# The long convolution's two VectorE accumulators in a PSUM bank in place of SBUF

## The chip, the cores and the metric

The kernel runs on one core of one Trainium2 chip. The metric is the device time of one execution in microseconds; the time before is the median of three runs. All arithmetic is float32, and every large matmul is done as three float32r passes (high times high, high times low, low times high), so that each weight needs a "high" and a "low" part made on the core.

## The reference, cut to what matters

A first block with two branches (a gated delta rule over 16 heads, and a GLU with a long depthwise convolution), then a second block of two layers. The change touches the convolution of the second branch alone:

```python
SEQ, CONV_CH, CONV_KERNEL = 256, 2048, 31
def causal_depthwise_conv(x, w):        # frame t sees t-K+1..t
    K = w.shape[0]
    xp = jnp.pad(x, ((0, 0), (K - 1, 0), (0, 0)))
    return lax.conv_general_dilated(xp, w[:, None, :], (1,), 'VALID', ..., feature_group_count=x.shape[-1])
...
u = jax.nn.glu(glu_in, axis=-1)
u = causal_depthwise_conv(u, w_dw[i]) + b_dw[i]
u = jax.nn.silu(layernorm(u, ln_g[i], ln_b[i])) * jax.nn.silu(z_b)
y_b = u @ w_br_b[i]
```

The 2048 channels are 16 groups of 128; a group lies with channels on the partitions and the 256 frames along the free dimension. Each frame is a sum of 31 products, plus the bias.

## The kernel before, in words

The kernel is a sequence of blocks. A block is one weight slab of 2048 rows by 512 columns, in 16 chunks of 128 rows, multiplied with 256 tokens (two tiles of 128). For each chunk ScalarE rounds the raw weights to `w_hi` (`hi_piece`, line 396), VectorE subtracts to get `w_lo` (`lo_piece`, line 402), and TensorE does six 512-column matmuls into one of two PSUM pairs (lines 422 to 424). ScalarE and VectorE work `AHEAD` = 6 chunks ahead of TensorE; `w_hi` holds 8 chunks, so a high piece waits for the chunk eight before it to be used. SyncE issues the weight loads of each quarter of a slab when its low pieces are made.

The order of everything else is written out by hand. A block has 32 half-steps `hs`, two to a chunk, and each engine walks them in order: at each one it does what the function for that engine lays on it and then, on VectorE, after each odd half-step one low piece. Blocks 0 to 15 are heads, blocks 16 to 31 are the convolution branch. Beside the projection of group j+1, the engines process group j (`group_pe`, `group_act`, `group_pool`, `group_dve`); group 0 runs beside the rule of head 15 as well, and group 15 beside the first block of the tail.

One group, by half-step:

- hs 0: ScalarE waits for the block's matmuls (`psum_ready`) and copies the pair to `bproj` (lines 770, 771); VectorE adds the gate bias (line 822).
- hs 1, 2: ScalarE takes the tanh of the gates (line 775); VectorE makes `glu2` and `z2b` (lines 831, 832).
- hs 5: TensorE waits for them (`glu_ready`) and transposes both into bank QA (line 760), in the midst of its stream of matmuls. ScalarE copies QA to `upad` and `zb` (lines 780, 782).
- hs 6 to 28: VectorE does 23 of the 31 taps, one per half-step, into two accumulators in turn: two `tensor_scalar` (lines 841, 843) and 21 `scalar_tensor_tensor` (line 847), each of which waits for the last write of its own accumulator. Inputs are `upad`, a tap weight per partition from `cwl`, and the accumulator.
- hs 8 to 22, even ones: ScalarE makes the other 8 products into `tap` (line 794), and GpSimd adds them up in `acc_p` with 7 `tensor_tensor` (line 815), each after the product it needs.
- hs 30, 31: VectorE adds its two accumulators (line 851), then `acc_p` (line 855), which gives `ub`. GpSimd stages the weights of the next group after line 851 (lines 806, 807).

PSUM is full: two pairs take four banks; QA and QB serve the heads' transposes, and RA and RB the rule. In the convolution blocks QA holds the transposes of hs 5. QB is last written for head 15, and next used in the norm of the tail.

Of the kernel before, what the change touches and what calls it, by code (L numbers as in the profile page):

```python
# [22 lines left out]
ALU = mybir.AluOpType  # L23
# [3 lines left out]
P = 128  # L27
D = 2048
S = 256
# [6 lines left out]
HEADS = 16  # L36
# [75 lines left out]
def program(nc, t, out, ctx):  # L112
# [16 lines left out]
    def sb(name, shape, dt=F32):  # L129

        h = nc.alloc_sbuf_tensor_at(name, shape, dt, offset=spot[0])
        spot[0] += (4 * int(np.prod(shape[1:])) + 31) // 32 * 32
        assert spot[0] <= nc.sbuf_usable_end
        return h
# [85 lines left out]
    ub = sb("ub", [P, KC, S])  # L220
# [3 lines left out]
    upad = sb("upad", [P, 2, LONG - 1 + S + 2])  # L224
# [2 lines left out]
    cwl = sb("cwl", [P, LONG + 1])  # L227
    assert spot[0] <= at_kq
    spot[0] = at_kq
    acc = sb("acc", [P, 2, S])  # L230
    glu2 = sb("glu2", [P, TT, P])
    assert spot[0] <= at_kq + 4 * TT * 3 * P
    spot[0] = at_ap
# [4 lines left out]
    acc_p = sb("acc_p", [P, S])  # L238
# [69 lines left out]
    QA, QB, RA, RB = (nc.alloc_psum_tensor(n, [P, NB], F32) for n in ("QA", "QB", "RA", "RB"))  # L308
# [6 lines left out]
    def both(x):  # L315

        return x.unsqueeze(1).broadcast_to([P, TT, P])
# [21 lines left out]
    s = {n: sem(n) for n in names}  # L339
# [11 lines left out]
    long_tap = [sem(f"long_tap{i}") for i in range(2)]  # L351
    tap_ready = [sem(f"tap_ready{i}") for i in range(2)]

    def reach(eng, which, value):

        if not isinstance(value, int) or value > 0:
            eng.wait_ge(which, value)
# [379 lines left out]
               .then_inc(s["oa_lo_done"], 1)  # L737


    POOL_TAPS = 8  # L740
    DVE_TAPS = LONG - POOL_TAPS

# [20 lines left out]
    def group_act(act, j, par, hs):  # L763
# [13 lines left out]
        if hs == 5:  # L777
# [5 lines left out]
               .then_inc(s["b_cols_taken"], 1)  # L783
        if 8 <= hs < 8 + 2 * POOL_TAPS and hs % 2 == 0:
            n = (hs - 8) // 2
# [6 lines left out]

            reach(act, s["pool_taps"], (POOL_TAPS - 1) * j + (max(n - 2, 1) if n >= 2 else 0))
            act.activation(tap[:, n % 2], upad[:, par, k:k + S], ACT.Copy, scale=cwl[:, k:k + 1])\  # L794
               .then_inc(tap_ready[n % 2], 1)

    def group_pool(pool, j, par):
# [5 lines left out]
        reach(pool, s["u_summed"], j)  # L803
        reach(pool, s["pool_taps"], (POOL_TAPS - 1) * j)
        taps = chan[:, CH_LONG:CH_END].rearrange("p (k g) -> p k g", g=KC)
        pool.tensor_copy(cwl[:, LONG:LONG + 1], chan[:, bass.ds(CH_BDW + j, 1)])
        pool.tensor_copy(cwl[:, 0:LONG], taps[:, :, bass.ds(j, 1)].rearrange("p k a -> p (k a)")).then_inc(s["cwl_staged"], 1)
        reach(pool, s["u_ready"], j)
        for n in range(1, POOL_TAPS):
            if n == 1:  # L810
                pool.wait_ge(tap_ready[0], POOL_TAPS // 2 * j + 1)
            else:
# [5 lines left out]
    def group_dve(dve, j, par, hs):  # L818
        if hs == 0:
            dve.wait_ge(psum_free, BLK_B + j + 1)  # L820
            dve.wait_ge(s["bg_loaded"], 16 * j + 16)
            dve.tensor_tensor(bproj[:, :, 3 * P:NB], bproj[:, :, 3 * P:NB], both(bg[:, :]), ALU.add)\
               .then_inc(s["gate_biased"], 1)
        if hs == 2:
            dve.wait_ge(s["b_tanh"], j + 1)
            if isinstance(j, int) and j == 0:
                dve.wait_ge(s["zs_ready"], HEADS)
                dve.wait_ge(s["oa_lo_done"], HEADS - 1)
                dve.wait_ge(s["pads_ready"], 4)
            reach(dve, s["b_cols"], j)  # L830
            dve.scalar_tensor_tensor(glu2[:, :, :], bth[:, :, 0], 1.0, bproj[:, :, 0:P], ALU.add, ALU.mult)
            dve.scalar_tensor_tensor(z2b[:, :, :], bth[:, :, 1], 1.0, bproj[:, :, 2 * P:3 * P], ALU.add, ALU.mult)\
               .then_inc(s["glu_ready"], 1)
        if 6 <= hs < 6 + DVE_TAPS:
            k = hs - 6
            src, a = upad[:, par, k:k + S], acc[:, k % 2]
            if k == 0:
                dve.wait_ge(s["b_cols_taken"], j + 1)
                dve.wait_ge(s["cwl_staged"], j + 1)
                reach(dve, s["u_ready"], j)  # L840
                dve.tensor_scalar(a, src, cwl[:, 0:1], cwl[:, LONG:LONG + 1], ALU.mult, ALU.add).then_inc(long_tap[0], 1)
            elif k == 1:
                dve.tensor_scalar(a, src, cwl[:, 1:2], None, ALU.mult).then_inc(long_tap[1], 1)
            else:
                n = (DVE_TAPS + 1 - k % 2) // 2
                dve.wait_ge(long_tap[k % 2], n * j + k // 2)
                dve.scalar_tensor_tensor(a, src, cwl[:, k:k + 1], a, ALU.mult, ALU.add).then_inc(long_tap[k % 2], 1)  # L847
        if hs == 30:
            dve.wait_ge(long_tap[0], (DVE_TAPS + 1) // 2 * (j + 1))
            dve.wait_ge(long_tap[1], DVE_TAPS // 2 * (j + 1))  # L850
            dve.tensor_tensor(acc[:, 0], acc[:, 0], acc[:, 1], ALU.add).then_inc(s["u_summed"], 1)
        if hs == 31:
            dve.wait_ge(s["u_summed"], j + 1)
            dve.wait_ge(s["pool_taps"], (POOL_TAPS - 1) * (j + 1))
            dve.tensor_tensor(ub[:, bass.ds(j, 1)].rearrange("p a n -> p (a n)"), acc[:, 0], acc_p[:, :], ALU.add)\
               .then_inc(s["u_ready"], 1)


# [789 lines left out]
    def beside_dve(dve, blk, hs):  # L1648
        at = 32 * (blk - BLK_GB) + hs
        done = blk - 1  # L1650
        if blk == BLK_GB:
            group_dve(dve, KC - 1, 1, hs)
# [275 lines left out]
    @block.vector  # L1928
    def _(dve):
        keys = lambda h, par, hs: keys_dve(dve, h, par, hs)  # L1930
        rule = lambda h, par, hs: rule_dve(dve, h, par, hs)
        group = lambda j, par, hs: group_dve(dve, j, par, hs)
        start_dve(dve)
        for q in range(AHEAD):
            lo_piece(dve, 0, q)
        dve_block(dve, 0, decays_beside(decays_first_dve, decays_dve, dve))
        dve.wait_ge(s["gc_stored"], 32)
        dve.wait_ge(s["pads_ready"], 3)
        dve_block(dve, 1, beside([(keys, 0, 0)]))
        heads = lambda h, i: dve_block(dve, h + i, beside([(rule, h + (i - 2), i), (keys, h + (i - 1), 1 - i)]), BESIDE_HEADS)  # L1940
        heads(2, 0)
        heads(2, 1)
        with dve.Fori(4, HEADS, 2) as h:
            for i in range(2):
                heads(h, i)
        dve_block(dve, BLK_B, beside([(rule, HEADS - 2, 0), (keys, HEADS - 1, 1)]))
        dve_block(dve, BLK_B + 1, beside([(rule, HEADS - 1, 1), (group, 0, 0)]))
        groups = lambda j, i: dve_block(dve, BLK_B + j + i, beside([(group, j + (i - 1), 1 - i)]))
        groups(2, 0)
        groups(2, 1)  # L1950
        with dve.Fori(4, KC, 2) as j:
            for i in range(2):
                groups(j, i)
        tail_dve(dve)
# [40 lines left out]
```

## Time and profile before

| | before |
|---|---|
| median of 3 runs | 2375.0 us (2374.96 to 2376.21) |
| the profiled execution's own time | 2376.49 us |
| its span | 2374.7 us |
| TensorE busy | 2283.1 us, 96% of the span |
| VectorE busy | 1577.0 us, 66% |
| ScalarE busy | 1267.3 us, 53% |
| GpSimd busy | 197.6 us, 8% |
| mean granted TensorE clock | 0.992 of full speed |

Busy shares are averages over stages that differ. In the page's 40 slices of the span (59 us each) VectorE stands at 9 tenths in the five slices from 712 to 1009 us, at 8 in the slice before them and the two behind, and at 4 to 7 in all the others; GpSimd is at 2 or 3 tenths from 653 to 1069 us and at 0 or 1 everywhere else. The stretch from 655 to 1055 us is the one with the long convolution.

### The profile page before, as it was taken

The page shows a single profiled execution, that of the slowest core. Times are in us where ns is not written, and L with a number is a line of the kernel's source. Part 1 is how long each engine was busy: PE and PEld are TensorE (multiplying, and loading weights), DVE is VectorE, ACT ScalarE, POOL GpSimd, SP SyncE. Part 2 cuts the span into 40 slices and gives each one's busy share as a digit, 9 for nine tenths or more (in the row PEclk, how much of TensorE's full clock was granted, in tenths as well). Part 3 has the DMA queues.
Part 4 walks back from the last instruction along what each step waited for, and adds up shares of the span by engine and source line. Part 5 has one row for each costly group of instructions (what it writes and reads, how often), then busy time and mean ns, then how long its engine had stood idle before and what let it go on. Part 6 is the DMA issues. An engine that isn't in the chain of part 4 may idle for free.

```text
span 2374.7 us, 32484 instructions
## 1 busy us (share of the span) xinstructions
PE 2283.1 (96%) x10958; PEld 1866.2 (79%) x10958; DVE 1577.0 (66%) x2913; ACT 1267.3 (53%) x2513; POOL 197.6 (8%) x357
## 2 busy tenths in 40 slices
PE   7999999999999989899999999999999989999997
PEld 5778878787777777777888888778878868888885
DVE  4766666666689999988565556565356664546665
ACT  4555555555566566557444555555445445455542
POOL 0001010010123223220000000000000000000000
PEclk9999999999999999999999999999999999999998
DMA  6634334344356666654665755556555545654462
GB/s 199 180 107 121 110 112 117 107 115 115 109 155 177 172 180 166 171 199 141 240 204 186 256 192 203 192 181 208 160 187 172 197 143 185 197 173 139 157 213 89
DMA packets 400615, 393.41 MB, mean 166 GB/s; under 512 B 15296, under 2 KB 284624, under 8 KB 398976
## 3 DMA queue, kind: packets, MB, share of 16 engines
q1 hardware_dynamic: 395968, 369.57, 50.0%
q0 software_dynamic: 4256, 20.38, 2.5%
q10 hardware_dynamic: 288, 2.10, 0.2%
q8 instruction: 63, 1.03, 0.2%
q14 instruction: 40, 0.33, 0.0%
HBM read 387.78 MB, written 4.21 MB: 165 GB/s over the span
## 4 chain that ended last, share of the span: by engine, by line
PE 76%; DVE 13%; issue 6%; ACT 3%; SPq 1%; DMA 1%; DVEq 0%; POOL 0%; ACTq 0%; POOLq 0%
PE pair L422 20%; PE pair L424 20%; PE pair L423 20%; DVE acc L847 5%; DVE w_lo L402 3%; PE RA L624 2%; PE RB L636 2%; PE RB L634 2%; PE QA L1208 1%; ACT w_hi L396 1%; PE RA L1224 1%; PE QA L480 1%; PE RB L628 1%; ACT bth L775 1%; PE QA L760 0%
## 5 line engine op out<-in xcount | busy, mean ns | idle before, releaser
L402 DVE TENSOR_TENSOR w_lo<-raw,w_hi 128x512 fp32r<-128x512 f32 x1376 | 942.7, 698 | 441.4 <-ACT w_hi L396 441.0
L396 ACT ACTIVATE w_hi<-raw 128x512 fp32r<-128x512 f32 x1376 | 839.5, 627 | 489.9 <-PE pair L424 479.9
L422 PE MATMUL pair<-w_hi,in_hi 128*128 128x512 f32 x2368 | 981.1, 414 | 12.4 <-DVE w_lo L402 6.6
L424 PE MATMUL pair<-w_hi,in_lo 128*128 128x512 f32 x2368 | 930.7, 393 | 0.0
L423 PE MATMUL pair<-w_lo,in_hi 128*128 128x512 f32 x2368 | 927.7, 392 | 0.0
L422 PEld LDWEIGHTS pair<-w_hi,in_hi 128*128 128x128 f32 x2368 | 448.7, 189 | 100.7 <-DVE w_lo L402 9.1
L424 PEld LDWEIGHTS pair<-w_hi,in_lo 128*128 128x128 f32 x2368 | 447.4, 189 | 96.7
L423 PEld LDWEIGHTS pair<-w_lo,in_hi 128*128 128x128 f32 x2368 | 449.4, 190 | 84.1 <-issue 4.8
L847 DVE SCALAR_TENSOR_TENSOR acc<-upad,cwl,acc 128x256 f32<-128x256 f32 x336 | 185.2, 587 | 0.0
L668 ACT ACTIVATE tri<-RB 128x512 f32<-128x512 f32 x96 | 54.1, 564 | 145.6 <-PE RB L636 145.6
L716 DVE TENSOR_TENSOR xm<-RA,const 128x256 f32<-128x256 f32 x96 | 40.8, 425 | 76.7 <-PE RA L624 76.7
L815 POOL TENSOR_TENSOR acc_p<-acc_p,tap 128x256 f32<-128x256 f32 x96 | 86.6, 902 | 45.6 <-ACT tap L794 42.5
L636 PE MATMUL RB<-tri,xm 128*128 128x128 f32 x384 | 71.7, 275 | 0.0
L624 PEld LDWEIGHTS RA<-tri,ap 128*128 128x128 f32 x384 | 56.4, 190 | 14.6 <-DVE tri L712 7.8
L634 PE MATMUL RB<-xm,tri 128*128 128x128 f32 x320 | 67.1, 292 | 0.0
L794 ACT ACTIVATE tap<-upad,cwl 128x256 f32<-128x256 f32 x128 | 63.8, 498 | 5.7 <-POOL acc_p L815 5.7
L634 PEld LDWEIGHTS RB<-xm,tri 128*128 128x128 f32 x320 | 49.4, 190 | 17.5 <-DVE xm L716 16.1
L574 DVE SCALAR_TENSOR_TENSOR conv<-conv_in,cw,conv 128x256 f32<-128x256 f32 x144 | 61.0, 479 | 0.8 <-ACT conv L499 0.8
L624 PE MATMUL RA<-tri,ap 128*128 128x128 f32 x384 | 59.9, 278 | 1.1
L636 PEld LDWEIGHTS RB<-tri,xm 128*128 128x128 f32 x384 | 58.1, 192 | 1.5 <-DVE xm L716 0.3
L422 PE MATMUL pair<-w_hi,mem_hi 128*128 128x512 f32 x128 | 51.6, 403 | 0.0
L422 PE MATMUL pair<-w_hi,ub_hi 128*128 128x512 f32 x128 | 50.5, 395 | 0.0
(372 smaller groups left out, 2095.6 us busy)
## 6 DMA issues: line engine op xcount, KB each, us to landing
raw<-in_w_in_dram SPq DMA_DIRECT2D x512, 256.0 KB, 3.5
raw<-in_w_in_dram SPq DMA_DIRECT2D x80, 1024.0 KB, 5.1
raw<-in_w_out_dram SPq DMA_DIRECT2D x48, 1024.0 KB, 5.0
raw<-in_w_kv_shared_dram SPq DMA_DIRECT2D x24, 1024.0 KB, 4.8
raw<-in_w_br_a_dram SPq DMA_DIRECT2D x16, 1024.0 KB, 5.0
raw<-in_w_br_b_dram SPq DMA_DIRECT2D x16, 1024.0 KB, 5.0
raw<-in_w_mem_kv_dram SPq DMA_DIRECT2D x16, 1024.0 KB, 4.8
raw<-in_w_ple_gate_dram SPq DMA_DIRECT2D x16, 1024.0 KB, 4.8
```

What stands on the lines that cost most here:

```text
L396: act.activation(w_hi[:, u % 2, q % UK], raw[:, u, q % UK], ACT.Copy).then_inc(hi_ready[u], 1)
L402: dve.tensor_tensor(w_lo[:, u % 2, q % UK], raw[:, u, q % UK], w_hi[:, u % 2, q % UK].bitcast(F32), ALU.subtract)\
L422: pe.matmul(o, xh, wh, start=(q == 0), stop=False)
L423: pe.matmul(o, xh, wl, start=False, stop=False)
L424: mm = pe.matmul(o, xl, wh, start=False, stop=(q == KC - 1))
L574: ins = dve.scalar_tensor_tensor(conv[:, c], conv_in[:, c, k:k + S], cw[:, k, c:c + 1], conv[:, c], ALU.mult, ALU.add)
L624: mm = pe.matmul(RA[:, tile * P:(tile + 1) * P], ap[:, par, tile, 0], tri[:, tile], start=True, stop=True)
L634: pe.matmul(RB[:, tile * P:(tile + 1) * P], tri[:, TT + tile], xm[:, tile], start=False, stop=True, skip_group_check=True)
L636: mm = pe.matmul(RB[:, (TT + tile) * P:(TT + tile + 1) * P], xm[:, tile], tri[:, TT + tile], start=False, stop=True, skip_group_check=True)
L794: act.activation(tap[:, n % 2], upad[:, par, k:k + S], ACT.Copy, scale=cwl[:, k:k + 1])\
L815: pool.tensor_tensor(acc_p[:, :], tap[:, 0] if n == 1 else acc_p[:, :], tap[:, n % 2], ALU.add)\
L847: dve.scalar_tensor_tensor(a, src, cwl[:, k:k + 1], a, ALU.mult, ALU.add).then_inc(long_tap[k % 2], 1)
```

## The change

`taps_sum` is another name for bank QB. The two accumulators are its halves of 256 columns. The SBUF tile `acc` shrinks to one accumulator, which takes the first of the two closing sums. The closing sums are ordered otherwise: first the even accumulator plus GpSimd's `acc_p` into `acc` (so the wait for `pool_taps` is now at hs 30 and the one for the odd accumulator at hs 31), then the odd accumulator plus `acc`. Group 0 also waits, before its first write, until ScalarE has read head 15's transposes out of QB.

```diff
-    acc = sb("acc", [P, 2, S])
+    acc = sb("acc", [P, S])
...
+    taps_sum = QB
...
-            src, a = upad[:, par, k:k + S], acc[:, k % 2]
+            src, a = upad[:, par, k:k + S], taps_sum[:, (k % 2) * S:(k % 2 + 1) * S]
             if k == 0:
                 dve.wait_ge(s["b_cols_taken"], j + 1)
                 dve.wait_ge(s["cwl_staged"], j + 1)
+                if isinstance(j, int) and j == 0:
+                    dve.wait_ge(s["kq_ready"], HEADS)
...
         if hs == 30:
             dve.wait_ge(long_tap[0], (DVE_TAPS + 1) // 2 * (j + 1))
-            dve.wait_ge(long_tap[1], DVE_TAPS // 2 * (j + 1))
-            dve.tensor_tensor(acc[:, 0], acc[:, 0], acc[:, 1], ALU.add).then_inc(s["u_summed"], 1)
+            dve.wait_ge(s["pool_taps"], (POOL_TAPS - 1) * (j + 1))
+            dve.tensor_tensor(acc[:, :], taps_sum[:, 0:S], acc_p[:, :], ALU.add).then_inc(s["u_summed"], 1)
         if hs == 31:
             dve.wait_ge(s["u_summed"], j + 1)
-            dve.wait_ge(s["pool_taps"], (POOL_TAPS - 1) * (j + 1))
-            dve.tensor_tensor(ub[:, ...], acc[:, 0], acc_p[:, :], ALU.add)\
+            dve.wait_ge(long_tap[1], DVE_TAPS // 2 * (j + 1))
+            dve.tensor_tensor(ub[:, ...], taps_sum[:, S:2 * S], acc[:, :], ALU.add)\
                .then_inc(s["u_ready"], 1)
```

## Rows read from the trace of the kernel before

**Rows 1.** Stretches: us, then busy of PE, PEld, DVE, ACT, POOL, clock, DMA share, GB/s
```profile
880.00:905.00 25.00, 22.46 (x95) 18.20 (x94) 23.92 (x44) 15.61 (x29) 7.94 (x9) 0.93 0.64 176
...
1155.00:1180.00 25.00, 25.00 (x112) 20.71 (x111) 13.95 (x21) 11.38 (x18) 0.70 (x1) 1.00 0.66 219
```

**Rows 2.** Waits of TensorE, 655 to 1060 us: total, times, longest
```profile
PE QA L760 <- DVE z2b L832: 28.6, 15, 2.6
PE pair L422 <- DVE ub L855: 1.4, 1, 1.4
```

**Rows 3.** Timeline of VectorE over one group: start us, us, instruction, [idle before]
```profile
760.23 0.41 DVE L841 TENSOR_SCALAR acc<-upad,cwl 128x256 f32<-128x256 f32 x1 [0.24 <-ACT zb L782]
...
762.82 1.36 DVE L847 SCALAR_TENSOR_TENSOR acc<-upad,cwl,acc 128x256 f32<-128x256 f32 x2
...
766.47 1.24 DVE L402 TENSOR_TENSOR w_lo<-raw,w_hi 128x512 fp32r<-128x512 f32 x1
...
771.95 0.87 DVE L847 SCALAR_TENSOR_TENSOR acc<-upad,cwl,acc 128x256 f32<-128x256 f32 x2
...
778.92 0.47 DVE L847 SCALAR_TENSOR_TENSOR acc<-upad,cwl,acc 128x256 f32<-128x256 f32 x1
...
781.50 0.45 DVE L822 TENSOR_TENSOR bproj<-bproj,bg 128x256 f32<-128x256 f32 x1
...
785.30 0.41 DVE L841 TENSOR_SCALAR acc<-upad,cwl 128x256 f32<-128x256 f32 x1 [0.39 <-ACT zb L782]
```

**Rows 4.** Timeline of GpSimd, the last add of the same group
```profile
770.28 0.86 POOL L815 TENSOR_TENSOR acc_p<-acc_p,tap 128x256 f32<-128x256 f32 x1 [0.69 <-ACT tap L794]
```

**Rows 5.** First and last start of one line's instructions, all groups: min/median/max ns
```profile
L847 DVE SCALAR_TENSOR_TENSOR acc<-upad,cwl,acc x336: 465/473/1043, 658.0 to 1053.6; 128x256 f32<-128x256 f32 x168
L841 DVE TENSOR_SCALAR acc<-upad,cwl x16: 412/414/418, 654.9 to 1034.9; 128x256 f32<-128x256 f32 x16
```

**Rows 6.** Timelines of TensorE and ScalarE around a group's start
```profile
783.84 0.43 PE L760 MATMUL QA<-const,glu 128*128 128x128 f32 x2 [2.53 <-DVE z2b L832]
784.24 0.47 PE L422 MATMUL pair<-w_hi,in_hi 128*128 128x512 f32 x1
...
771.82 0.63 ACT L396 ACTIVATE w_hi<-raw 128x512 fp32r<-128x512 f32 x1 [0.73 <-PE pair L424]
775.90 0.63 ACT L396 ACTIVATE w_hi<-raw 128x512 fp32r<-128x512 f32 x1 [0.73 <-PE pair L424]
777.34 0.69 ACT L770 ACTIVATE bproj<-pair,small 128x512 f32<-128x512 f32 x1 [0.81 <-PE pair L424]
```

**Rows 7.** Timelines of GpSimd and VectorE beside the rule of head 15
```profile
660.95 0.74 POOL L815 TENSOR_TENSOR acc_p<-tap 128x256 f32<-128x256 f32 x1 [17.80 <-ACT tap L794]
661.13 0.42 DVE L716 TENSOR_TENSOR xm<-RA,const 128x256 f32<-128x256 f32 x1 [1.30 <-PE RA L624]
...
664.86 0.73 POOL L815 TENSOR_TENSOR acc_p<-acc_p,tap 128x256 f32<-128x256 f32 x1 [0.19 <-ACT tap L794]
664.98 1.29 DVE L847 SCALAR_TENSOR_TENSOR acc<-upad,cwl,acc 128x256 f32<-128x256 f32 x2
```

**Rows 8.** VectorE groups of the whole kernel by shape: busy us, mean ns
```profile
L574 DVE SCALAR_TENSOR_TENSOR conv<-conv_in,cw,conv 128x256 f32<-128x256 f32 x144 | 61.0, 479 | 0.8 <-ACT conv L499 0.8
L594 DVE TENSOR_SCALAR vb<-tok,hst 128x128 f32<-128x128 f32 x32 | 8.9, 278 | 0.0
L569 DVE COPY conv_in<-QB 128x256 f32<-128x256 f32 x16 | 6.6, 414 | 0.0
L843 DVE TENSOR_SCALAR acc<-upad,cwl 128x256 f32<-128x256 f32 x16 | 5.6, 348 | 0.0
L724 DVE COPY o_t<-RB 128x128 f32<-128x128 f32 x16 | 4.5, 281 | 0.0
L1273 DVE RECIPROCAL st<-st 128x2 f32<-128x2 f32 x20 | 3.3, 164 | 8.5 <-ACT sc L1241 8.5
L891 DVE SCALAR_TENSOR_TENSOR in_lo<-QA,chan,in_hi 128x256 fp32r<-128x256 f32 x4 | 1.7, 478 | 3.5 <-ACT in_hi L878 3.5
```

More of the change, by code:

```diff
@@ L849, in group_dve @@
             dve.wait_ge(long_tap[0], (DVE_TAPS + 1) // 2 * (j + 1))
-            dve.wait_ge(long_tap[1], DVE_TAPS // 2 * (j + 1))
-            dve.tensor_tensor(acc[:, 0], acc[:, 0], acc[:, 1], ALU.add).then_inc(s["u_summed"], 1)
+            dve.wait_ge(s["pool_taps"], (POOL_TAPS - 1) * (j + 1))
+            dve.tensor_tensor(acc[:, :], taps_sum[:, 0:S], acc_p[:, :], ALU.add).then_inc(s["u_summed"], 1)
         if hs == 31:
             dve.wait_ge(s["u_summed"], j + 1)
-            dve.wait_ge(s["pool_taps"], (POOL_TAPS - 1) * (j + 1))
-            dve.tensor_tensor(ub[:, bass.ds(j, 1)].rearrange("p a n -> p (a n)"), acc[:, 0], acc_p[:, :], ALU.add)\
+            dve.wait_ge(long_tap[1], DVE_TAPS // 2 * (j + 1))
+            dve.tensor_tensor(ub[:, bass.ds(j, 1)].rearrange("p a n -> p (a n)"), taps_sum[:, S:2 * S], acc[:, :], ALU.add)\
                .then_inc(s["u_ready"], 1)
```

## The prediction

> **What bounds the kernel now.** I read the 40 slices first (where is VectorE full?), then busy times of single stretches, then TensorE's waits, then the timelines of one group. In the tail TensorE is busy all 25 us of a 25 us stretch and VectorE 14. In the convolution stage it is the other way: VectorE 23.9 of 25, TensorE 22.5 [rows 1]. TensorE loses its time in one place: 15 times it waits for `z2b` of line 832, 28.6 us in all, before the transposes of half-step 5 [rows 2]. ScalarE, at 15.6 of 25, is not it.
>
> One group shows why. Line 841 starts at 760.23 and again at 785.30: a period of 25.07 us, and VectorE is hardly ever idle in it [rows 1, 3]. From 771.95 to 778.92 VectorE does five chunks (two taps and one low piece each) in 6.97 us, 1.394 us a chunk. Before that, from 762.82 to 771.95, it does only four chunks, in 9.13 us where 5.58 would do: 3.55 us lost [rows 3]. This is when GpSimd adds: its last add of the group begins at 770.28 [rows 4]. A tap that takes 473 ns in the median goes up to 1043 [rows 5], a low piece to 1.24 us [rows 3]. So each GpSimd add that meets VectorE costs it about 0.57 us (1043 - 473), once. Seven adds would be 4.0 us; 3.55 was lost.
>
> Which operands make the two collide? Beside the rule of head 15 there are cases side by side. Line 716 (one input in PSUM, one in SBUF) starts at 661.13, within GpSimd's add of 660.95 to 661.69, and takes 0.42 us, its usual length. The pair of line 847 (both tensors in SBUF) at 664.98, within the add of 664.86, takes 1.29 us where a clean pair takes 0.87 [rows 3, 7]. After the change a tap has one tensor in SBUF, `upad`, and one in PSUM, as line 716 has.
>
> **The change part by part.** Sums are made per group.
>
> VectorE's own loop, clean. From line 841 to line 822: 781.50 - 760.23 = 21.27, less the 3.55 = 17.72 us. From line 822 through the tanh, `z2b`, the transposes and ScalarE's copies back to line 841: 785.30 - 781.50 = 3.80 us [rows 3]. Together 21.52.
>
> The two `tensor_scalar`. Line 843 takes 348 ns for 256 columns where the same kind with 128 takes 278: 0.55 ns a column. Copies out of PSUM take 281 for 128 and 414 for 256: 1.04 ns a column [rows 8]. I take it that a one-source operation with its output in PSUM goes at the second slope: 0.49 x 256 = 0.13 us more each, 0.27 us for two. Loop: 21.79. The ends are 0 and 0.27.
>
> The 21 `scalar_tensor_tensor`. For a read from PSUM the trace has the same instruction: line 891 takes 478 ns with one tensor in PSUM, line 574 takes 479 with both in SBUF, at the same 256 columns with a weight per partition [rows 8]. So the read costs nothing. No VectorE instruction of this trace writes PSUM. Lower end of that price: 0, as for the read (a gain isn't excluded, but with both orders of read alike I give it no weight). Upper end: the fixed part of an operation is at most the 164 ns that line 1273 takes for 2 columns [rows 8]; half of it, the writing half, doubled: 82 ns more. That is 1.9 us for 23 taps. I take 10 ns, nearest to the row of line 891: 0.2 us. Loop: 22.0.
>
> The Trainium skill states a rule against this change: "Perfetto Trace Analysis", section "Optimizing Scalar/DVE Operations", gives VectorE about 60 ns of access overhead per instruction on SBUF and about 125 ns on PSUM. By it 23 taps would cost 1.5 us more a group and the loop would be 23.3 before leftovers. The rows of lines 891 and 574 do not bear it out for reads; for writes no row here decides.
>
> What is left of the collisions. Low pieces still have both inputs in SBUF, and one of them has been 1.24 us [rows 3]. But taps now run free, 0.79 us of each 1.394 us chunk. GpSimd gets one product per chunk of TensorE, 1.36 us apart ((775.90 - 771.82)/3 for ScalarE's high pieces, which come one to a chunk) [rows 6]. An add that comes during a low piece waits for it and then has 0.79 us of taps for its 0.57; only one that comes in the last 0.57 of the taps delays the next low piece, and by that delay it moves the adds after it into the harmless part. I count one such hit a group: 0.5 us. Ends: 0, and 3.9 (seven hits). Loop: 22.5.
>
> TensorE's own floor. 16 chunks x 1.36 = 21.76 us, and 784.24 - 783.84 = 0.40 for the transposes: 22.17 us a group [rows 6]. Its present 2.53 us of waiting [rows 6] shrinks to some 0.4. This is next: below 22.17 VectorE's gain is worth nothing. ScalarE's `bproj` to VectorE's `z2b` is hidden under half-steps 0 to 5 (six times 0.68, 4.1 us of matmuls, against 3.7: two copies of 0.69 and the 2.34 from line 822 at 781.50 to the transposes at 783.84 [rows 3, 6]). The granted clock is 0.93 in this stretch of the stage and 1.00 in the tail's, where TensorE never waits [rows 1]; 0.07 x 25 is 1.75 us of TensorE's time, which at present the wait for VectorE hides. With waits of 0.4 us I expect the clock not to fall. I set the mean period at 22.6, a tenth above the loop for unevenness.
>
> Edits at no cost. The wait for `pool_taps` moves one half-step earlier, to hs 30. The last GpSimd add is over at 771.14 and VectorE gets there at about 779.9, 8.8 us later [rows 3, 4]; less 3, the order still holds. Were it late, all low pieces behind it would wait, and TensorE six chunks on. The closing sums have one PSUM and one SBUF input in place of two in SBUF; same length. The wait for head 15's copies is for work a block old. The smaller `acc` moves `glu2`, which changes nothing.
>
> **Sum.** Line 841 of group 5 starts at 785.30 and that of group 15, the last, at 1034.9 [rows 3, 5]: ten periods of 24.96 us. From group 1 to group 15 there are 14 such periods: 14 x (24.96 - 22.6) = 33.0 us. Group 15 has no following group, but TensorE waits 1.4 us for its `ub` [rows 2]: VectorE's way from line 841 to line 855 loses 3.55 and gets 1.0 back, a gain of 2.5. Group 0 lies beside the rule, whose chain of short waits (1.30 us before line 716) sets its pace [rows 7]; collisions there are fewer: 1 us. Sum 36 us. Against the profiled execution's own 2376.5: 2340.4. The median is 1.5 below that execution: I predict 2339.5 for the median.
>
> **The rivals.**
>
> A, the fixed price on PSUM writes is real, about 60 ns (between the ends 0 and 82). Loop 21.79 + 0.5 + 25 x 0.06 = 23.8. Gain 14 x 1.1 + 1.2 + 0.5 = 17: 2358. At 82 ns: 24.3, a gain of 10, 2365. For it: nothing shows a PSUM write. Against: reads are free. The Trainium skill's rule above comes out here: 65 ns in place of 60, 2359.
>
> B, a low piece takes most of the hits (four of seven, 2.3 us). Loop 21.99 + 2.3 = 24.3: 2365. For it: low pieces do collide. Against: the adds align themselves as above.
>
> C, nothing is removed: the tap weight in `cwl` is an SBUF input too, and line 716 has none, so that a tap still collides. The loop gets only the 0.27 + 0.2: 14 x 0.47 = +7 at most, about 2380; without the 0.2, 2379. In effect the change doesn't do what it says. For it: no row has a tap weight, a PSUM tensor and a GpSimd add together.
>
> D, slower: a tap reads and writes the same bank, and if the bank serves only one of them at a time, each of 256 columns takes 1.04 ns twice: 267 ns more a tap, 5.6 us a group. Loop 21.79 + 0.5 + 5.6 = 27.9; 14 x 3 + 5 for the ends = +47: 2422. It decides against the change from (24.96 - 22.3)/21 = 0.13 us per tap. Against: TensorE's matmuls add into a bank at 512 columns in 0.227 us (1.36/6), four times VectorE's rate, reading and writing it.
>
> **How the numbers follow.** My forecast (2331 to 2348): 0.60. A: 0.14. B: 0.08. C: 0.09. D: 0.09. The lower end is a TensorE floor in every group (14 x 2.76 + 3.5 = 42, and 2 us more for group 0): 2331. The upper end takes in A with both ends: 2366. What lies beyond, C and D, is 0.18. A measurement of this kernel tells 0.2% (4.7 us) from no change. Faster: forecast, A, B = 0.82. Same: most of C = 0.08. Slower: D and the rest of C = 0.10.
>
> **What would show it.** Line 847 has a median of 470 to 490 ns and hardly any above 600; GpSimd's adds keep about 0.74 and are stretched only by low pieces. Low pieces over 1.0 us: about one a group. Line 843 goes from 348 to about 480. Line 841 comes every 22.3 to 22.9 us. TensorE's 28.6 us of waiting before line 760 falls to under 8, and its clock stays at 1.00. Wrong would be: taps of 550 ns throughout (A), of 740 (D), or still up to 1.04 us (C); a period under 22.2 is excluded by TensorE.

## The result and the profile after

The changed kernel takes 2335.5 us (median of 4 runs, 2334.1 to 2336.2) against 2375.6 (2375.0 to 2376.8) in the same comparison: a ratio of 0.983, 95% interval 0.9813 to 0.9847. I had predicted 2339.5. The profiled execution has a span of 2333.9 us, 40.8 less than the one before.

The page's first part and its line 847, now 850:

```profile
PE 2270.8 (97%) x10958; PEld 1859.8 (80%) x10958; DVE 1524.9 (65%) x2913; ACT 1268.1 (54%) x2513; POOL 213.6 (9%) x357
...
L850 DVE SCALAR_TENSOR_TENSOR QB<-upad,cwl,QB 128x256 f32<-128x256 f32 x336 | 147.6, 482 | 0.0
```

The same number of instructions; VectorE is busy 52 us less. The stretches of the convolution stage (columns as in [rows 1]):

```profile
805.00:830.00 25.00, 25.00 (x114) 20.64 (x113) 23.40 (x51) 17.45 (x34) 10.83 (x12) 1.00 0.70 191
880.00:905.00 25.00, 25.00 (x114) 20.71 (x113) 22.74 (x50) 16.65 (x32) 8.73 (x11) 1.00 0.75 201
```

TensorE is now busy all the time and at its full clock, as in the tail; VectorE, at 22.7 to 23.4 of 25, is not. The waits of TensorE from 650 to 1060 us, as in [rows 2]:

```profile
PE QA L761 <- DVE z2b L833: 0.2, 1, 0.2
```

28.6 us of waiting have become 0.2. VectorE's timeline over one group, beside [rows 3]:

```profile
752.54 0.55 DVE L844 TENSOR_SCALAR QB<-upad,cwl 128x256 f32<-128x256 f32 x1 [0.42 <-ACT zb L783]
752.99 0.48 DVE L846 TENSOR_SCALAR QB<-upad,cwl 128x256 f32<-128x256 f32 x1
...
753.98 0.88 DVE L850 SCALAR_TENSOR_TENSOR QB<-upad,cwl,QB 128x256 f32<-128x256 f32 x2
...
760.29 0.70 DVE L402 TENSOR_TENSOR w_lo<-raw,w_hi 128x512 fp32r<-128x512 f32 x1
...
767.82 0.49 DVE L850 SCALAR_TENSOR_TENSOR QB<-upad,cwl,QB 128x256 f32<-128x256 f32 x1
...
771.04 0.43 DVE L823 TENSOR_TENSOR bproj<-bproj,bg 128x256 f32<-128x256 f32 x1 [0.56 <-ACT bproj L772]
...
774.84 0.55 DVE L844 TENSOR_SCALAR QB<-upad,cwl 128x256 f32<-128x256 f32 x1 [0.41 <-ACT zb L783]
```

From 753.98 to 767.82 there are ten chunks of 1.384 us without a single slow one. VectorE now gets to line 823 with 0.56 us to spare and waits for ScalarE's copies of the pair. ScalarE in turn waits for TensorE:

```profile
769.63 0.69 ACT L771 ACTIVATE bproj<-pair,small 128x512 f32<-128x512 f32 x1 [0.80 <-PE pair L424]
```

So the bound has changed hands. GpSimd's adds of the same group, beside [rows 4]:

```profile
757.65 1.17 POOL L816 TENSOR_TENSOR acc_p<-acc_p,tap 128x256 f32<-128x256 f32 x1 [0.21 <-ACT tap L795]
758.98 2.61 POOL L816 TENSOR_TENSOR acc_p<-acc_p,tap 128x256 f32<-128x256 f32 x2 [0.16 <-POOL acc_p L816]
761.75 2.61 POOL L816 TENSOR_TENSOR acc_p<-acc_p,tap 128x256 f32<-128x256 f32 x2 [0.16 <-POOL acc_p L816]
```

Four of the group's seven now last 1.3 us, where the clean length is 0.73. An add that starts while a low piece runs (758.98, low piece from 758.91) is not done until the taps behind it. The order of giving way has turned round: it is mostly GpSimd that waits, which costs no time here, where VectorE waited before. The margin is thin: the adds of 758.98 and 761.75 end, two by two, at 761.59 and 764.36, each about 0.1 us before a low piece starts (761.68 and 764.45).

Groups of lines over all groups (min/median/max ns, first and last start), of the changed kernel:

```profile
L850 DVE SCALAR_TENSOR_TENSOR QB<-upad,cwl,QB x336: 469/482/493, 658.0 to 1012.4; 128x256 f32<-128x256 f32 x168
...
L402 DVE TENSOR_TENSOR w_lo<-raw,w_hi x227: 673/684/696, 700.5 to 1014.2; 128x512 fp32r<-128x512 f32 x114
...
L816 POOL TENSOR_TENSOR acc_p<-acc_p,tap x96: 728/1227/1312, 664.0 to 1007.6; 128x256 f32<-128x256 f32 x96
```

The adds in the kernel before:

```profile
L815 POOL TENSOR_TENSOR acc_p<-acc_p,tap x96: 727/821/1289, 663.9 to 1046.5; 128x256 f32<-128x256 f32 x96
```

The longest tap of 336 is 493 ns; it was 1043 [rows 5]. From 700 us on, no low piece is over 696 ns. The median add went from 821 to 1227 ns.

Where the 40.8 us lie, by line 822/823 in both traces: group 1 starts at 682.31 before and 682.32 after, so group 0 gave nothing. Group 15 starts at 1031.4 (first-to-last start of line 822) and here at 993.22:

```profile
682.32 0.43 DVE L823 TENSOR_TENSOR bproj<-bproj,bg 128x256 f32<-128x256 f32 x1 [0.33 <-ACT bproj L772]
...
993.22 0.43 DVE L823 TENSOR_TENSOR bproj<-bproj,bg 128x256 f32<-128x256 f32 x1 [0.38 <-ACT bproj L772]
```

Fourteen periods of 24.94 us are now fourteen of 22.21: 38.2 us. The other 2.6 came with group 15.

### The profile page after: what moved, and what is told of

It is laid out like the page before. It is cut to its first block, busy times and chain, and to the rows that moved or that the text cites. A ratio compares the mean times of both kernels' runs of the same rounds, so it can differ in the third digit from the quotient of the medians.

```text
span 2333.9 us, 32484 instructions
## 1 busy us (share of the span) xinstructions
PE 2270.8 (97%) x10958; PEld 1859.8 (80%) x10958; DVE 1524.9 (65%) x2913; ACT 1268.1 (54%) x2513; POOL 213.6 (9%) x357
## 4 chain that ended last, share of the span: by engine, by line
PE 91%; DVE 5%; ACT 2%; issue 1%; SPq 1%; DMA 1%; POOL 0%; DVEq 0%; ACTq 0%; POOLq 0%
PE pair L424 25%; PE pair L422 25%; PE pair L423 25%; PE RA L624 2%; PE RB L636 2%; PE RB L634 2%; DVE w_lo L402 1%; PE QA L1211 1%; PE RA L1227 1%; PE QA L480 1%; PE RB L628 1%; PE QB L1296 0%; PE QA L870 0%; SPq L370 0%; PE RA L1450 0%
## 5 line engine op out<-in xcount | busy, mean ns | idle before, releaser
L402 DVE TENSOR_TENSOR w_lo<-raw,w_hi 128x512 fp32r<-128x512 f32 x1376 | 927.6, 688 | 441.8 <-ACT w_hi L396 441.4
L850 DVE SCALAR_TENSOR_TENSOR QB<-upad,cwl,QB 128x256 f32<-128x256 f32 x336 | 147.6, 482 | 0.0
L816 POOL TENSOR_TENSOR acc_p<-acc_p,tap 128x256 f32<-128x256 f32 x96 | 110.6, 1152 | 27.3 <-ACT tap L795 20.6
L716 DVE TENSOR_TENSOR xm<-RA,const 128x256 f32<-128x256 f32 x96 | 40.8, 425 | 77.0 <-PE RA L624 77.0
```

Of the source, the lines that this page charges most:

```text
L402: dve.tensor_tensor(w_lo[:, u % 2, q % UK], raw[:, u, q % UK], w_hi[:, u % 2, q % UK].bitcast(F32), ALU.subtract)\
L816: pool.tensor_tensor(acc_p[:, :], tap[:, 0] if n == 1 else acc_p[:, :], tap[:, n % 2], ALU.add)\
```

## The experiments

In each, the kernel before ran beside the experiment on the same chip and took 2376.4 to 2377.9 us there; ratios are to it. "Period" is the mean of the 14 from group 1 to group 15, from one gate-bias add (line 822 of the kernel before) to the next.

**Is it the collisions, or PSUM?** GpSimd's adds cut to one column, in the kernel before:

```diff
+            pool.memset(acc_p[:, :], 0.0)
...
-            pool.tensor_tensor(acc_p[:, :], tap[:, 0] if n == 1 else acc_p[:, :], tap[:, n % 2], ALU.add)
+            pool.tensor_tensor(acc_p[:, 0:1], tap[:, 0, 0:1] if n == 1 else acc_p[:, 0:1], tap[:, n % 2, 0:1], ALU.add)
```

> The kernel before (accumulators in SBUF), with each of GpSimd's seven adds cut to one of its 256 columns; the rest of acc_p stays zero, so seven of the eight products that ScalarE makes are left out of the sum in most columns. All waits and instruction counts stay. My theory (the gain is the end of the collisions between GpSimd's adds and VectorE's two-SBUF-input instructions): VectorE's loop falls from 24.94 to 21.5 us a group, under TensorE's floor of 22.2, so the period is 22.2 and the time 2375.6 - 14 x 2.73 - 2.6 = 2335, within 2 us of the changed kernel, with the accumulators still in SBUF; taps of 473 ns with none over 550. Rival 1 (a tap is cheaper with its accumulator in PSUM, whatever GpSimd does): nothing moves, 2374 to 2377. Rival 2 (half by collisions, half by PSUM): 2355.

Measured: 2334.9 us, ratio 0.9816 (0.980 to 0.983). Taps in its trace, all in SBUF:

```profile
L848 DVE SCALAR_TENSOR_TENSOR acc<-upad,cwl,acc x336: 466/475/481, 658.7 to 1013.0; 128x256 f32<-128x256 f32 x168
```

The whole gain is there with no accumulator in PSUM, and the period is the changed kernel's, 22.21 us. Both rivals fall. The gain of the change is the end of the collisions, up to TensorE's floor.

**Is anything left of them?** The same cut in the changed kernel.

> The changed kernel (accumulators in PSUM) with the same cut of GpSimd's adds to one column. My theory: the adds cost nothing any more, since no low piece meets them and TensorE sets the pace, so 2335.5, within 1.5 us of the changed kernel. Rival (some collisions are left, on the low pieces, and still cost time): 2 to 6 us faster than the changed kernel, 2330 to 2333.

Measured: 2335.7 us (2335.4 to 2336.5), the changed kernel's 2335.5 again, and the same period, 22.21. Whatever GpSimd still does to VectorE is covered.

**Half the cure.** Only the even accumulator in PSUM:

```diff
+    odd = sb("odd", [P, S])
...
-            src, a = upad[:, par, k:k + S], taps_sum[:, (k % 2) * S:(k % 2 + 1) * S]
+            src, a = upad[:, par, k:k + S], odd[:, :] if k % 2 else taps_sum[:, 0:S]
...
-            dve.tensor_tensor(ub[:, ...], taps_sum[:, S:2 * S], acc[:, :], ALU.add)\
+            dve.tensor_tensor(ub[:, ...], odd[:, :], acc[:, :], ALU.add)\
```

> The changed kernel with the odd accumulator back in SBUF; only the even one lies in PSUM. VectorE's chunk is then even tap (free, 0.39 us), odd tap (collides), low piece (collides, 0.60). My theory, an add holds what both need for about 0.57 us and whoever comes first has it: the free stretch of 0.39 us is 0.18 shorter than an add, so each of seven adds costs at least 0.18 us and the loop is 21.6 + 1.3 to 2.2 = 22.9 to 23.8: 14 x 0.7 to 1.6 above the changed kernel, 2345 to 2358. Rival (what counts is the share of instructions that collide, gains add up tap by tap): half the gain, 2355 to 2356, or, if TensorE's floor cuts it, somewhat lower. Rival (one accumulator in PSUM is enough to keep out of the adds' way): 2336.

Measured: 2348.7 us, ratio 0.987 (0.986 to 0.989), period 23.14: in my range, and below the proportional rival's 2355. VectorE's timeline in it (line 851 in both forms, low piece now line 403):

```profile
757.64 0.57 DVE L851 SCALAR_TENSOR_TENSOR odd<-upad,cwl,odd 128x256 f32<-128x256 f32 x1
...
759.13 0.57 DVE L851 SCALAR_TENSOR_TENSOR odd<-upad,cwl,odd 128x256 f32<-128x256 f32 x1
759.63 1.23 DVE L403 TENSOR_TENSOR w_lo<-raw,w_hi 128x512 fp32r<-128x512 f32 x1
760.78 0.48 DVE L851 SCALAR_TENSOR_TENSOR QB<-upad,cwl,QB 128x256 f32<-128x256 f32 x1
```

The tap in PSUM is never slow; five odd ones of this group are 0.10 us longer than clean (0.57 against 0.47), which I read as the remainder of an add that the even tap doesn't cover, where I had reckoned with 0.18; and two low pieces of the group take a full hit (1.23 us, here at 759.63).

**The order of the closing sums alone.** In the kernel before, `acc_p` into the even accumulator at half-step 30 and the odd one at 31, with the waits of the change.

> The kernel before with only the new order of the two closing sums (the wait for GpSimd's taps at half-step 30, that for the odd accumulator at 31), accumulators in SBUF. My theory: GpSimd is done 8.8 us earlier, so nothing: 2375.6, within 1.5. Rival (the earlier wait costs, and the change would be faster without it; or the order is part of the gain): over 3 us away from 2375.6.

Measured: 2377.7 us beside 2377.9, ratio 0.9999 (0.9989 to 1.0009). This part is neutral.

**Can low pieces be hit?** The changed kernel with each add done twice:

```diff
+    acc_q = sb("acc_q", [P, S])
...
+            pool.tensor_tensor(acc_q[:, :], tap[:, 0] if n == 1 else acc_p[:, :], tap[:, n % 2], ALU.add)
             pool.tensor_tensor(acc_p[:, :], tap[:, 0] if n == 1 else acc_p[:, :], tap[:, n % 2], ALU.add)\
```

> The changed kernel with GpSimd doing each add twice, first into a scratch tile: 14 adds a group in place of 7, output unchanged. GpSimd then has two adds per chunk, about 1.5 us of work for a chunk of 1.38 us. My theory (each add holds the shared access about 0.57 us, low pieces need it too, and the changed kernel is spared only because one add fits between two low pieces): the second add starts near the end of the 0.79 us of taps and each of some seven low pieces waits about 0.5 us; VectorE's loop goes from 21.7 to 25 us, over TensorE's 22.2, so 14 x 2.8 = 40 us more, 2370 to 2380; taps stay at 482 ns, low pieces go up to 1.24 us. Rival (low pieces always win over GpSimd, who has to wait): nothing, 2334 to 2337, low pieces at 684 ns throughout.

Measured: 2367.2 us, ratio 0.996 (0.995 to 0.998), period 24.29: 3 us under my range. VectorE, then GpSimd:

```profile
766.88 1.13 DVE L403 TENSOR_TENSOR w_lo<-raw,w_hi 128x512 fp32r<-128x512 f32 x1
767.94 0.87 DVE L852 SCALAR_TENSOR_TENSOR QB<-upad,cwl,QB 128x256 f32<-128x256 f32 x2
768.72 1.13 DVE L403 TENSOR_TENSOR w_lo<-raw,w_hi 128x512 fp32r<-128x512 f32 x1
...
766.74 0.73 POOL L818 TENSOR_TENSOR acc_p<-acc_p,tap 128x256 f32<-128x256 f32 x1
767.63 0.99 POOL L817 TENSOR_TENSOR acc_q<-acc_p,tap 128x256 f32<-128x256 f32 x1 [0.16 <-POOL acc_p L818]
768.58 0.73 POOL L818 TENSOR_TENSOR acc_p<-acc_p,tap 128x256 f32<-128x256 f32 x1
```

The second add starts at 766.74 and 768.58, 0.14 us ahead of a low piece at 766.88 and 768.72, and each low piece is 0.45 us longer. Taps between them keep 0.87 for two. So low pieces do not win over GpSimd; the changed kernel is spared because it has one add per chunk, as expected. The price was lower than I had said: six low pieces a group are hit, at 0.46 us each, where I had some seven at 0.5. The mean of the low pieces is 851 ns against 684, times 16 is 2.7 us a group; 21.7 + 2.7 is 24.4, near the 24.29.

**How much slack has VectorE now?** The changed kernel with `POOL_TAPS = 6`, so 25 taps on VectorE.

> The changed kernel with 25 taps on VectorE and 6 on GpSimd's side, in place of 23 and 8. Two taps are 0.78 us more on VectorE's loop of 21.7 or so; TensorE's floor is 22.2. My theory (about 0.5 us of slack is left on VectorE): the period goes to 22.5, 14 x 0.3 = 4 us and a bit for the last group: 2339 to 2343. Rival (VectorE has still a margin of a microsecond or more): 2335.5, no change. Rival (VectorE still sets the period): 0.78 x 15 = 12 us, 2347.

Measured: 2340.2 us (2340.15 to 2341.7), ratio 0.985 (0.983 to 0.986), period 22.51. As expected: about 0.5 us of slack, and beyond it VectorE sets the pace once more.

**The price of PSUM itself.** Spare taps on VectorE until it is the bound by far, with no adds to collide with; once all in SBUF, once all in PSUM:

```diff
                 dve.scalar_tensor_tensor(a, src, cwl[:, k:k + 1], a, ALU.mult, ALU.add).then_inc(long_tap[k % 2], 1)
+                if not (isinstance(j, int) and j == 0):
+                    ...
+                    ins = dve.scalar_tensor_tensor(EXTRA, src, cwl[:, k:k + 1], EXTRA, ALU.mult, ALU.add)
```

> To measure what an accumulator in PSUM costs where VectorE sets the period and nothing collides: the kernel before with GpSimd's adds cut to one column (as in the first experiment, so seven of eight of ScalarE's products are left out of most columns), and in groups 1 to 15 after each of the 21 later taps a spare one into a scratch tile in SBUF (one tensor_scalar, then 20 scalar_tensor_tensor). Loop 21.5 + 0.27 + 20 x 0.395 = 29.7 us; 14 x 7.5 and 7 for the last group above 2335: 2440 to 2455. This is the base for the next kernel; both theories give it the same.

> The same as the one before with both accumulators and the scratch tile in PSUM (scratch in bank RA), so 41 scalar_tensor_tensor and 3 tensor_scalar a group read or write PSUM. My theory (a write to PSUM costs nothing per scalar_tensor_tensor, a tensor_scalar costs 0.13 us more): 14.7 x 0.4 = 6 us above the kernel before it, 3 to 9. Rival A of the prediction (60 ns fixed for each): 15 x 44 x 0.06 = 40 us above it. Rival (PSUM is the faster place, 482 ns long but shorter from start to start): the 6 us are made up for, equal or below.

Measured: 2455.3 us in SBUF (2454.8 to 2455.7), 0.3 above my range, a period of 30.00; 2457.9 in PSUM (2455.9 to 2458.4), a period of 30.15. The difference is 2.5 us, just under the 3 to 9 I had given. Groups of VectorE from 705 to 1000 us, first SBUF, then PSUM:

```profile
L850 DVE SCALAR_TENSOR_TENSOR acc<-upad,cwl,acc 128x256 f32<-128x256 f32 x205 | 98.3, 479 | 0.0
L856 DVE SCALAR_TENSOR_TENSOR vb<-upad,cwl,vb 128x256 f32<-128x256 f32 x195 | 93.5, 480 | 0.0
```

```profile
L853 DVE SCALAR_TENSOR_TENSOR QB<-upad,cwl,QB 128x256 f32<-128x256 f32 x204 | 98.1, 481 | 0.0
L859 DVE SCALAR_TENSOR_TENSOR RA<-upad,cwl,RA 128x256 f32<-128x256 f32 x194 | 93.2, 481 | 0.0
...
L849 DVE TENSOR_SCALAR QB<-upad,cwl 128x256 f32<-128x256 f32 x10 | 4.8, 478 | 0.0
```

The period is 0.15 us longer, where the three `tensor_scalar` alone account for 0.39. The 41 taps must have given back 0.24, some 6 ns each: the truth lies between my theory (a write costs nothing, 6 us) and the rival by which the shorter steps make up for all of it. Rival A, at 40 us, is out. The difference of the two medians is of the size of what a chip's runs differ by, so the sign of the 6 ns rests more on the chunks of the traces (1.394 us clean in SBUF [rows 3], 1.384 in PSUM) than on these two times.

**Does the price of a hit go with the length of the add?** The kernel before with adds of 128 columns in place of 256.

> The kernel before (accumulators in SBUF) with GpSimd's seven adds cut to 128 of their 256 columns; the other half of acc_p stays zero, so seven of the eight products are left out of the sum in half the columns. A clean add takes 0.73 us for 256 columns and 0.19 for one, so about 0.46 for 128, and a hit should cost VectorE 0.57 - 0.27 = 0.30 us in place of 0.57. My theory (a hit lasts as long as the add still reads, so its price goes with the add's columns): seven hits of 0.30 are 2.1 us, VectorE's loop 21.5 + 2.1 = 23.6, period 1.4 above TensorE's 22.2: 2335 + 14 x 1.4 + 1 = 2356, between 2348 and 2362 as more or fewer adds meet VectorE; slowed taps at 0.75 to 0.80 us in place of 1.04. Rival (a hit costs the same whatever the add's length): 2372 to 2377. Rival (the half adds fit in between, no loss): 2335.

Measured: 2346.6 us, ratio 0.987 (0.986 to 0.989), period 22.94. VectorE's lines in it:

```profile
L848 DVE SCALAR_TENSOR_TENSOR acc<-upad,cwl,acc x336: 468/476/714, 657.2 to 1022.8; 128x256 f32<-128x256 f32 x168
...
L402 DVE TENSOR_TENSOR w_lo<-raw,w_hi x214: 674/682/952, 704.5 to 1009.7; 128x512 fp32r<-128x512 f32 x107
```

Its timeline, a pair with both taps hit and a low piece that is hit:

```profile
757.67 1.29 DVE L848 SCALAR_TENSOR_TENSOR acc<-upad,cwl,acc 128x256 f32<-128x256 f32 x2
...
763.69 0.95 DVE L402 TENSOR_TENSOR w_lo<-raw,w_hi 128x512 fp32r<-128x512 f32 x1
```

A hit costs 0.21 us on a tap (1.29 against 0.87 for a pair, two hits) and 0.27 on a low piece (0.95 against 0.68). With whole adds it costs 0.49 and 0.56 (the section on the prediction shows them). So a hit becomes cheaper by 0.28, and the add is shorter by 0.27 (its shortest is 457 ns in place of 727): the price does go with the add's length, and neither rival holds. My 0.30 was too high, and the time came out 1.4 us under my range: there are again seven hits a group, mostly six on taps and one on a low piece, 1.53 us in all. On a clean loop of 21.4 (24.94 less 3.55 in the kernel before) that gives 22.9, the measured period.

## Why the prediction was right

**The bound and the cause.** Right, and shown: VectorE set the period because GpSimd's adds held it up, and taking the adds away (first experiment) or their meeting with the taps (the change) gives the same period of 22.21 us.

**The price of a hit.** I took 0.57 us, from the length of the slowest tap, and found 4.0 us for seven adds where 3.55 was lost. The lengths overlap with the next instruction, and 1043 ns is the longest of 336. The kernel before has these rows beside those of [rows 3], in the same group:

```profile
764.70 1.84 DVE L847 SCALAR_TENSOR_TENSOR acc<-upad,cwl,acc 128x256 f32<-128x256 f32 x2
...
767.63 1.35 DVE L847 SCALAR_TENSOR_TENSOR acc<-upad,cwl,acc 128x256 f32<-128x256 f32 x2
768.90 1.24 DVE L402 TENSOR_TENSOR w_lo<-raw,w_hi 128x512 fp32r<-128x512 f32 x1
770.07 1.36 DVE L847 SCALAR_TENSOR_TENSOR acc<-upad,cwl,acc 128x256 f32<-128x256 f32 x2
```

A clean pair is 0.87 and a clean low piece 0.68. With the pair at 762.82 (1.36) and the low piece at 766.47 (1.24) of [rows 3] that is five hits on taps at 0.49 (two of them in the pair of 764.70) and two on low pieces at 0.56: seven, one for each add, and 3.55 us. By 0.49, the half cure's remainder is 0.49 - 0.39 = 0.10, which is what its odd taps show.

**The clean loop.** I had 17.72 + 3.80 = 21.52 us. The changed kernel's is 771.04 - 0.56 - 752.54 = 17.94 and 774.84 - 771.04 = 3.80, 21.74 in all, with the 0.27 for the `tensor_scalar` in it. That term was right: 0.27 said, 0.26 measured (546 and 478 ns against 414 and 348 [rows 5, 8]).

**The price per tap.** I took 10 ns. The duration is 9 longer (482 against 473), but from start to start a tap is some 5 ns shorter, so this term was 0.2 us and is -0.1. By an estimate from the Trainium skill's overhead of 125 ns against 60 ("Perfetto Trace Analysis", "Optimizing Scalar/DVE Operations") 41 taps and 3 others would have been 2.9 us a group dearer; the pair of kernels with spare taps shows 0.15.

**The leftover hits.** This is the step that was mis-sized. I counted one hit of 0.5 us a group and added a tenth for unevenness, 22.6; there are none from group 1 on, and the period is TensorE's own 22.2. Fourteen times 0.39 is 5.5 us, more than the whole error of the forecast (4.0). The reason I gave, that adds fall in behind low pieces by themselves, was right and stronger than I had used it: the first add already starts in a low piece (755.01 in the trace, low piece from 754.76). That the adds would keep about 0.74 us was wrong: their median is 1227 ns.

**TensorE's floor.** 22.17 computed, 22.21 measured. Nothing of the gain below it was to be had, and none was got: the kernels with tiny adds have no better time in either form.

**The clock.** The stretch of [rows 1] at 0.93 was not typical: of the 16 stretches of 25 us from 655 to 1055 us in the kernel before, 5 have 0.93 and 11 have 1.00, though TensorE stands still before `z2b` in all but the first of the 16. Two rows of the kernel before, a stretch like that of [rows 1] and one microsecond after the wait of 2.53 us [rows 6]:

```profile
830.00:855.00 25.00, 22.46 (x102) 18.36 (x101) 23.99 (x45) 15.39 (x29) 7.37 (x9) 1.00 0.65 176
...
786.00:787.00 1.00, 1.00 (x4) 0.71 (x4) 1.00 (x3) 1.00 (x3) 0.00 (x0) 0.50 1.08 319
```

So the 1.75 us that I had the wait hide were there in a third of the groups only, as 3.4 us at half clock. In the changed kernel the stretches of the stage have 1.00, as I expected.

**Group 15 and group 0.** 2.5 said, 2.6 measured. The 2.6 are by subtraction: until TensorE's first matmul on `ub` in the tail group 15 gains 2.9 us, and 0.3 are lost behind it. For group 0 I had said 1 us and there is none. VectorE waits 1.31 us for line 624 before one `xm` where it had waited 0.88: the 0.43 us it was ahead went into that wait, since TensorE's chain of the rule sets that block's pace. One low piece there is still hit (1.14 us at 674.40), at no cost in time.

**The sum as written.** Its three terms, 33.0, 2.5 and 1, make 36.5 and not 36, and 1.5 below the profiled execution's figure is then 2338.5 for the median, not 2339.5. The measured 2335.5 lies in the range either way.

**The rivals.** A: out by the spare taps. B: none of the seven hits went to a low piece, though the doubled adds show that they can. C: no tap is over 493 ns, so a tap weight in SBUF beside one SBUF tensor doesn't collide. D: taps would have been 740 ns, and they are 482. (The argument against D had a slip: 0.227 us for 512 columns is 0.44 ns a column, 2.3 times VectorE's rate of 1.04 and not four times.) The edits costed at nothing (the order, the earlier wait) were nothing.

The Trainium skill has this as a rule in "SBUF — State Buffer", section "Who interferes with whom": a VectorE instruction with two SBUF inputs contends with a GpSimd instruction that reads SBUF, and one with at most one SBUF input doesn't, outside VectorE's two-port modes. All runs here agree, in their numbers above. Of the two-port modes the section says that whoever issues first has the shared ports for the whole instruction. For two SBUF inputs the runs here show less than the whole: an add of 0.73 us delays a tap by 0.49 and a low piece by 0.56, one of 0.46 by 0.21 and 0.27, and one of 0.19 (a single column) not at all, since no tap of that kernel is over 481 ns.

## What to carry to other kernels

When a VectorE instruction shows two durations, look at what GpSimd does at that moment, and count SBUF tensors among the inputs: with one of them moved to a free PSUM bank, a two-input instruction costs the same here (482 ns long against 473, and 5 ns less from start to start) and is no longer held up. Count what a hit costs per loop and compare with the next engine's floor before hoping for more; here 3.55 us of hits a group were worth 2.73, because TensorE's own 22.2 us then set the period. One-source instructions are the exception: with the output in PSUM they lost 0.13 us each at 256 columns.

## What the runs showed that I had not expected

- GpSimd and VectorE fell into step: with taps in PSUM the later adds of a group come every 1.38 us, VectorE's chunk, and last 1.3 us each, and from 700 us on not one low piece was hit.
- An add that waits is drawn out, not VectorE: with adds of one column GpSimd's longest takes 1151 ns where its shortest takes 189, while no tap of that kernel is over 481 ns. With the accumulators in PSUM the median of the same adds is 192. First SBUF, then PSUM:

```profile
L816 POOL TENSOR_TENSOR acc_p<-acc_p,tap x96: 189/983/1151, 664.7 to 1007.9; 128x1 f32<-128x1 f32 x96
```

```profile
L817 POOL TENSOR_TENSOR acc_p<-acc_p,tap x96: 190/192/768, 664.7 to 1007.8; 128x1 f32<-128x1 f32 x96
```

- An accumulator that is read and written in the same PSUM bank by each instruction, the next one working in the other half of the bank, shows no loss from start to start: a chunk takes 1.384 us against 1.394 in SBUF.
